# A third product on unscaled rows at each of four model-wide norms, and the scaling of the rows spread over it

## The reference

```python
def rmsnorm(x, g):
    xf = x.astype(jnp.float32)
    y = xf * lax.rsqrt(jnp.mean(xf * xf, axis=-1, keepdims=True) + EPS)
    return (y * g.astype(jnp.float32)).astype(x.dtype)
...
        hn = rmsnorm(h, mix_norm_g[l])
        proj = hn @ w_in[l]
        q_a, k_a, v_a, cq, ckv, k_pe = jnp.split(proj, IN_SPLITS, axis=-1)
...
        h = h + conv_glu(rmsnorm(h, ffn_norm_g[l]), w_gate[l], w_up[l], conv_w[l], conv_b[l], w_down[l])
...
        h = rmsnorm_2(x, norm_mix_g[l]) * (1.0 + sc_m) + sh_m
        proj = h @ w_in[l]
        a_b, a_c, a_x, q, f_logit, i_in, g_out, gate_a, gate_b = jnp.split(proj, split_idx, axis=-1)
...
        h2 = rmsnorm_2(x, norm_ffn_g[l]) * (1.0 + sc_f) + sh_f
        ff = (jax.nn.silu(h2 @ w_ffn_gate[l]) * (h2 @ w_ffn_up[l])) @ w_ffn_down[l]
```

## Time and profile before

| | |
|---|---|
| median of 3 runs | 2751.41 us (2748.62 to 2752.8) |
| the profiled execution | 2753.61 us, of it 2752.2 us span |
| PE busy | 97% of the span, mean granted clock 0.989 |
| DVE, ACT, POOL busy | 67%, 45%, 12% |

### The profile page before, as it was taken

The page is one execution under the profiler, slowest core; times in us unless marked ns, Lnnn a source line. Parts: engine busy times, 40 slices in busy tenths (PEclk is TensorE's granted clock), DMA queues, the critical chain, the costliest instruction groups (busy, mean ns, idle before and its releaser), DMA issues.

```text
span 2752.2 us, 51365 instructions
## 1 busy us (share of the span) xinstructions
PE 2677.2 (97%) x22052; PEld 2636.4 (96%) x22052; DVE 1836.5 (67%) x2578; ACT 1248.1 (45%) x1943; POOL 324.8 (12%) x526
## 2 busy tenths in 40 slices
PE   6999999899999999998999999999989999999998
PEld 6988889899999999998999999999989999999998
DVE  5656568777777777776888667766876445454444
ACT  5556555544433444445434443334544433344443
POOL 1110101111111111221000001111221000000001
PEclk9999999999999999999999999999999999999999
DMA  6433445688888888885444568886767556555553
GB/s 200 120 117 94 125 144 176 202 271 263 271 280 283 268 272 273 266 283 177 142 152 153 185 228 270 276 271 218 256 204 252 184 179 189 193 190 184 184 182 125
DMA packets 500084, 571.22 MB, mean 208 GB/s; under 512 B 26704, under 2 KB 473424, under 8 KB 499856
## 3 DMA queue, kind: packets, MB, share of 16 engines
q1 hardware_dynamic: 467968, 463.76, 51.9%
q0 software_dynamic: 31600, 103.80, 11.6%
q10 hardware_dynamic: 288, 0.36, 0.0%
HBM read 565.77 MB, written 2.54 MB: 206 GB/s over the span
## 4 chain that ended last, share of the span: by engine, by line
PE 86%; DVE 7%; ACT 4%; issue 1%; DMA 0%; POOL 0%; SPq 0%; DVEq 0%; ACTq 0%
PE ps L681 27%; PE ps L682 27%; PE ps L683 26%; DVE wl L1780 3%; ACT wh L1273 2%; PE ps L976 1%; PE ps L810 1%; DVE lr L1976 1%; DVE nx L1884 0%; ACT lp L1446 0%; DMA raw<-in_w_in 0%; PE ps L783 0%; DVE sqt L1884 0%; PE ps L835 0%; PE ps L836 0%
## 5 line engine op out<-in xcount | busy, mean ns | idle before, releaser
L1780 DVE TENSOR_TENSOR wl<-raw,wh 128x1024 fp32r<-128x1024 f32 (+1 forms) x894 | 1058.5, 1200 | 630.4 <-ACT wh L1273 626.2
L681 PE MATMUL ps<-xx,wh 128*128 128x256 f32 (+2 forms) x4848 | 1385.8, 286 | 29.2 <-DVE xx L1861 16.3
L682 PE MATMUL ps<-xx,wh 128*128 128x256 f32 (+2 forms) x4848 | 1366.4, 282 | 0.0
L683 PE MATMUL ps<-xx,wl 128*128 128x256 f32 (+2 forms) x4848 | 1363.1, 281 | 0.0
L1273 ACT ACTIVATE wh<-raw 128x1024 fp32r<-128x1024 f32 (+1 forms) x894 | 882.2, 1029 | 621.8 <-PE ps L683 612.3
L681 PEld LDWEIGHTS ps<-xx,wh 128*128 128x128 f32 x4848 | 918.0, 189 | 38.4 <-DVE wl L1780 21.9
L682 PEld LDWEIGHTS ps<-xx,wh 128*128 128x128 f32 x4848 | 918.9, 190 | 1.7 <-issue 1.0
L683 PEld LDWEIGHTS ps<-xx,wl 128*128 128x128 f32 x4848 | 918.4, 189 | 0.0
L681 PE MATMUL ps<-hid,wh 128*128 128x256 f32 x1408 | 393.9, 280 | 0.0
L682 PE MATMUL ps<-hid,wh 128*128 128x256 f32 x1408 | 393.7, 280 | 0.0
L683 PE MATMUL ps<-hid,wl 128*128 128x256 f32 x1408 | 392.8, 279 | 0.0
(11 more groups left out here) (366 smaller groups left out, 2387.4 us busy)
## 6 DMA issues: line engine op xcount, KB each, us to landing
raw<-in_w_in SPq DMA_DIRECT2D x118, 1024.0 KB, 5.3
ada_raw<-in_w_ada POOLq DMA_DIRECT2D x384, 256.0 KB, 4.7
raw<-in_w_gate SPq DMA_DIRECT2D x44, 1024.0 KB, 6.4
raw<-in_w_up SPq DMA_DIRECT2D x44, 1024.0 KB, 7.0
raw<-in_w_ffn_gate SPq DMA_DIRECT2D x44, 1024.0 KB, 5.1
raw<-in_w_ffn_up SPq DMA_DIRECT2D x44, 1024.0 KB, 5.6
raw<-in_w_down SPq DMA_DIRECT2D x32, 1024.0 KB, 6.6
raw<-in_w_ffn_down SPq DMA_DIRECT2D x32, 1024.0 KB, 5.5
```

Of the source, the lines that this page charges most:

```text
L681: pe.matmul(dst, h[:, c, o:o + w], x[:, 0, k, g.t0:g.t1], start=(k == 0), stop=False)
L682: pe.matmul(dst, h[:, c, o:o + w], x[:, 1, k, g.t0:g.t1], start=False, stop=False)
L683: m = pe.matmul(dst, l[:, c, o:o + w], x[:, 0, k, g.t0:g.t1], start=False, stop=end)
L1780: dve.tensor_tensor(wl[i % NS][:, part], raw[i % NR][:, part], wh[i % NS][:, part].bitcast(F32), ALU.subtract).then_inc(s_lo, 1)
```

## The change

At each of the four norms the third product is made raw too: `ckv` at N_IN, the second gate product of both feed-forward parts, and `i` at N_MIX2. The first product on scaled rows is the fourth one: `kpe`, which has 64 outputs and so 48 matmuls, the second up product, and `g`. For that

- the raw rows of three norms get buffers that outlast a third product (`raw_ffn` in two parts inside the space of `hid`, `raw_mix` for six chunks; chunks 6 to 15 of N_MIX2 still lie in `xx`, so that ScalarE may write the scaled high half of such a chunk only when the third product has passed it);
- `SCALE_AT` becomes a list with a pump for each chunk: one scaling a pump from pump 8 on for the feed-forward norms, where before four chunks took three pumps. ScalarE's high half of a chunk comes two pumps behind its scaling. VectorE's low half of an even chunk stays four chunks behind its scaling. GpSimd has its own count for odd chunks, three pumps behind the scaling;
- the third product's result is multiplied with `rstd` when it is read, by VectorE: two more reads for each norm (`unscaled`), with `keep_shift` for the shift product in the second block. `ckv` and `i`, which ScalarE copied out of PSUM, are now read by VectorE (for `i` ScalarE adds the shift behind it);
- `ada` is started or resumed one pair of products later in both feed-forward parts;
- the level masks are loaded to another place.

```diff
 def paced(n, i):
     if n in RAW_NORMS:
-        return pause((0, 1, 0, 2)[i % 4])
+        return pause(SCALE_AT[n][i + 1] - SCALE_AT[n][i] if i + 1 < KD else 2)
     return pause(i % 4 == 3)
...
-RAW_SHARED = {N_IN: [], N_FFN1: list(range(8, 16)), N_MIX2: list(range(16)), N_FFN2: []}
+RAW_SHARED = {N_IN: [], N_FFN1: [], N_MIX2: list(range(6, 16)), N_FFN2: []}
...
-RAW_KEY2 = {N_IN: ("cq", 1), N_FFN1: (1, "up", 0, 0), N_MIX2: ("f", 0), N_FFN2: (2, "up", 0, 0)}
+RAW_LAST = {N_IN: ("ckv", 0), N_FFN1: (1, "gate", 0, 1), N_MIX2: ("i", 0), N_FFN2: (2, "gate", 0, 1)}
...
-SCALE_AT = {N_IN: 10, N_FFN1: 8, N_MIX2: 8, N_FFN2: 6}
+SCALE_AT = {N_IN: [10, 11, 12, 13, 14, 15, 16, 17, 17, 18, 19, 20, 20, 21, 22, 23],
+            N_FFN1: [8 + i for i in range(16)],
+            N_MIX2: [10, 11, 12, 14, 16, 18, 19, 20, 21, 21, 22, 23, 24, 24, 25, 26],
+            N_FFN2: [8 + i for i in range(16)]}
...
-            gemm(("ckv", 0), normed(N_IN))
+            gemm_raw(N_IN, ("ckv", 0))
             lanes.start("latent", latent())
-            gemm(("kpe", 0))
+            gemm(("kpe", 0), normed(N_IN))
...
+                        elif f == 0 and g == 1:
+                            gemm_raw(n, (b, "gate", f, g))
+                            gemm((b, "up", f, g), normed(n))
                             if b == 1:
                                 lanes.start("ada", ada(), slow=True)
                             else:
                                 lanes.resume("ada")
...
-                    if p == 0 and n in "qf":
+                    if p == 0 and n != "g":
                         gemm_raw(N_MIX2, (n, p), square_sums if n == "q" else None)
...
                 if n in RAW_NORMS:
-                    yield from pause(SCALE_AT[n] + 1)
+                    yield from pause(SCALE_AT[n][1] + 3)
...
                     root(n)
-                    yield from pause(SCALE_AT[n] + 1 - ROOT_AT[n])
+                    yield from pause(SCALE_AT[n][0] + 2 - ROOT_AT[n])
...
+            dve.wait_ge(s_slab, done(("ckv", 0)))
+            for j in range(2):
+                unscaled(("ckv", 0), j, T, ckv[:, j, :])
             lanes.start("latent", latent())
```

More of the change, by code:

```diff
@@ L280 @@
 RAW_KEY = {N_IN: ("cq", 0), N_FFN1: (1, "gate", 0, 0), N_MIX2: ("q", 0), N_FFN2: (2, "gate", 0, 0)}
-RAW_T0 = {N_IN: Q0, N_FFN1: Q0, N_MIX2: Q0, N_FFN2: 0}
-RAW_T1 = {N_IN: T, N_FFN1: T, N_MIX2: T, N_FFN2: T - Q0}
-RAW_SHARED = {N_IN: [], N_FFN1: list(range(8, 16)), N_MIX2: list(range(16)), N_FFN2: []}
+RAW_T0 = {N_IN: Q0, N_FFN1: Q0, N_MIX2: 0, N_FFN2: 0}
+RAW_T1 = {N_IN: T, N_FFN1: T, N_MIX2: T - Q0, N_FFN2: T - Q0}
+RAW_SHARED = {N_IN: [], N_FFN1: [], N_MIX2: list(range(6, 16)), N_FFN2: []}
 RAW_LAG = {N_FFN1: {g: ([2 * g - 2, 2 * g - 1] if g < 7 else [12, 13, 14, 15]) for g in range(1, 8)},
@@ L470, in raw_half @@
                 return raw_in[:, h, i, :]
-            if n == N_FFN2:
-                return raw_ffn[:, h, i, :]
-            return xb[:, h, i, :] if n == N_FFN1 and i < 8 else xx[:, h, i, :]
+            if n == N_MIX2:
+                return raw_mix[:, h, i, :] if i < 6 else xx[:, h, i, Q0:T]
+            return raw_ffn[i // 8][:, h, i % 8, :]
         def raw_body(n, h, i):
@@ L481, in raw_shift @@
         def raw_shift(n, h):
[L482 to L485 removed]
+            if n == N_MIX2:
+                parts = [raw_mix[:, h, :, 0:META - Q0], xx[:, h, 6:KD, Q0:META]]
+            else:
+                parts = [x[:, h, :, 0:META - Q0] for x in raw_ffn]
+            m, c = (6, 0) if n == N_MIX2 else (8, 48)
+            cols = [mod[:, c:c + m], mod[:, c + m:c + KD]]
+            return [(x, y.unsqueeze(2).to_broadcast([P, k, META - Q0])) for x, y, k in zip(parts, cols, (m, KD - m))]
         def root_of(n):
@@ L624, in gemm_raw @@
                 t0, t1 = RAW_T0[n], RAW_T1[n]
+                if key == ("ckv", 0):
+                    t0 = 0
                 if key == (1, "up", 0, 0):
@@ L630, in gemm_raw @@
                 if NORM_SHIFT[n]:
-                    pe.wait_ge(s_shl, 1 if n == N_MIX2 else 2)
+                    pe.wait_ge(s_shl, 2 if n == N_MIX2 else 4)
                 for i in g.slabs:
@@ L652, in gemm_raw @@
                             m.then_inc(s_slab, 1)
-                        elif key == RAW_KEY2[n] and k in RAW_SHARED[n]:
+                        elif key == RAW_LAST[n] and k in RAW_SHARED[n]:
                             m.then_inc(s_passed, 1)
@@ L1070, in norm_lows @@
                     yield from paced(n, i)
+                    if n in RAW_NORMS and i + 1 < KD:
+                        yield from paced(n, i + 1)
             def squares(n, i):
@@ L1318, in pair_squares @@
                                 act.wait_ge(*last_use(("cq", g), j))
+                        act.wait_ge(s_slab, done(("ckv", 0)))
                     if n == N_CKV:
@@ L2338, in vector_program @@
                             dve.wait_ge(s_fq, j + 1)
+                            unscaled(key, j, SEQ, ssq["ab"[j]][:, 0:SEQ], META - Q0)
+                    if p == 0 and n == "i":
+                        dve.wait_ge(s_slab, done(key))
+                        for j in range(2):
+                            keep_shift(key, j, 4 + j)
+                            dve.wait_ge(s_fs, j + 1)
                             unscaled(key, j, SEQ, ssq["ab"[j]][:, 0:SEQ], META - Q0)
```

66 lines of the change are left out of this document (36 added, 30 removed).

## The result

The changed kernel takes 2722.57 us (median of 4 runs, 2720.61 to 2724.4) beside 2750.01 us (4 runs, 2746.86 to 2752.8) for the kernel before on the same chip. The ratio is 0.9898, 95% interval 0.9886 to 0.9910. The forecast was 2713, a gain of 38.6 us; measured are 28 by the ratio, 27.4 by the medians. The direction holds; the gain was forecast 10 us too large. The profiled execution took 2723.26 us with a span of 2721.9.

A forecast was written before the change was run, and what follows sets the result against it. TensorE, busy 97% of the span, was taken as the bound, with 46.9 us lost in four stalls; less 6.3 of remaining stalls and 2.0 of clock, the gain was 38.6 us, median 2713, range 2702 to 2731.

The forecast's parts named there:

- all is covered: Rival, 10%: waits for wh vanish and the key rotation's wait goes too, gain 49.0 us, so 2702.
- N_FFN1, chunk 12: Fourth product at N_FFN1: chunk 12 wanted at 31.4 us, its low half done at 34.1, a stall of 2.7 us.
- collisions: At N_FFN1, VectorE low halves beside GpSimd ones take 0.87 instead of 0.42 us; two on the path, 0.9 us.
- Stalls and the clock behind them: All four norms: 6.3 us of stalls left, plus 2.0 us for one half-clock stretch of 4 us.
- N_MIX2: stall of 1.6 us forecast: Second slab of g: chunk 12's low half waits behind wl, with four ScalarE roundings ahead of its wh; 1.6 us.
- N_FFN2: 1.0 forecast: As at N_FFN1, but third read-out 0.9 instead of 3.0 us and one more rounding per odd chunk: stall 1.0 us.
- N_IN: 1.0 forecast: At kpe, chunk 14 is wanted at 5.2 us and VectorE needs 5.5 to 6.5 before it: stall 1.0 us.
- It is not pushed into a wait later: At N_FFN2 the 2.7 us wait for ada_acc goes; ada's last group ends inside that part's first half.
- the forecast case: Main case, 62%: 2706 to 2719 us, its stalls between 3 and 12 us.
- the backlog is larger: Rival, 19%: all eight odd low halves collide, 14.4 us, and the clock falls at each stall, 8 us; gain 18, 2733.
- The wait moves: Rival, 5%: VectorE reaches wl late, TensorE waits for wl at line 648 or 681; gain under 5 us, 2748.
- the ring of five: Rival, 4%, slower: a scaling waits for GpSimd's low half five chunks back; 64 us lost instead of 46.9, 2768.

The follow-up runs named there:

- the best version: Changed kernel with later scalings earlier at three norms (N_MIX2's one pump more), all low halves on VectorE, ada's first start as before: 2710.26 us, 0.9843 of the kernel before.
- order: Changed kernel with other pump numbers alone, later scalings earlier at N_FFN1, N_MIX2 and N_FFN2: 2715.58 us, 0.9867 of the kernel before.
- after_again: The changed kernel unaltered, run once more as a control: 2724.65 us, 0.9897 of the kernel before.
- ada1: Changed kernel with ada in the first feed-forward part started behind the second product, as in the kernel before: 2720.72 us, 0.9887 of the kernel before.
- undo_ffn1: Changed kernel with N_FFN1 alone put back to two raw products, and ada's start with it: 2729.36 us, 0.9919 of the kernel before.
- lows_dve: Changed kernel with all 16 low halves of the four norms on VectorE, none on GpSimd: 2718.38 us, 0.9878 of the kernel before.
- the undo kernels: Changed kernel with one norm put back to two raw products: N_IN 2728.78, N_FFN1 2729.36, N_MIX2 2732.21, N_FFN2 2733.39 us.

## Why the prediction was right and where it was off

Between the profiled executions the gain is 2753.6 − 2723.3 = 30.3 us, 8.3 less than the 38.6 of the sum. The terms that it lies in: 5.0 us of stalls and half clock left at three norms, 2.0 given back between N_MIX2 and N_FFN2, and 1.1 at N_IN, which is inside the play of that part. The medians are 27.4 apart, since the profiled run before stood above its median by more than the one after.

- **What bounds the kernel: right.** TensorE stood still for low halves, and taking these waits away gave the time. The case "all is covered", 2702, is 8 us below the median of the best version.
- **The third raw product costs nothing: right**, 95 matmuls in 11 us.
- **N_FFN1, chunk 12: right in place and cause, low in size.** The second product starts at 482.3 us, chunk 12 is wanted at 513.5, 31.2 on (forecast 31.4), and its low half is done at 517.3, 35.0 on (forecast 34.1). Timeline of VectorE:

```profile
506.89 1.22 DVE L1798 TENSOR_TENSOR wl<-raw,wh 128x1024 fp32r<-128x1024 f32 x1
508.03 0.87 DVE L1881 TENSOR_TENSOR xx<-sqt,xx 128x258 fp32r<-128x258 f32 x1
...
512.33 0.41 DVE L1851 TENSOR_TENSOR ssq_a<-ps,rstd 128x258 f32<-128x258 f32 x1
...
515.32 1.22 DVE L1798 TENSOR_TENSOR wl<-raw,wh 128x1024 fp32r<-128x1024 f32 x1
516.45 0.87 DVE L1881 TENSOR_TENSOR xx<-nx,xx 128x258 fp32r<-128x258 f32 x1
```

  The read-out and its taps take 512.33 to 515.32, the forecast 3.0 us, and then a `wl` piece stands before the low half. In `order`, where the last low halves and their roundings stand ahead of it, the stall is gone, so their place is the cause. **The term of this ledger that was mis-sized is that of collisions**: two on the path, 0.9 us, were taken; 7 of 8 even low halves took 0.86 to 0.87 us, 3.1 us. It was partly made up by shorter waits for `wh`, 2.0 us where 3.0 were taken, and by the nine `wl` pieces, which follow each other at 1.14 us (506.89 to 508.03) and not at 1.2.
- **Stalls and the clock behind them.** The windows lose 5.2, 3.6 and 3.5 us, 12.3 in all, against 5.3 of stalls and 2.0 of clock in the forecast. Of the 5.0 us between, which are the largest part of what is missing, 3.6 are longer stalls (8.9 us) and 1.4 is the rest, for the most part half clock. One stretch of half clock, 3.4 us long, came at N_FFN1 (from 516.9, in the wait of 3.8 us) and one at N_FFN2 (from 2005.1, behind a wait of 1.9); the wait of 2.3 us at N_MIX2 brought none. In `after_again`, the same program, it was the other way round: a stretch at N_MIX2 behind a wait of 2.8 us, none at N_FFN2 behind one of 1.9. Its windows at N_MIX2 and N_FFN2:

```profile
1250.00:1290.00 40.00, 36.00 (x291) 35.64 (x290) 33.34 (x53) 27.18 (x45) 9.43 (x9) 0.96 0.54 177
1990.00:2030.00 40.00, 37.49 (x317) 37.11 (x316) 32.16 (x46) 24.45 (x37) 8.27 (x12) 1.00 0.67 220
```

- **N_MIX2: stall of 1.6 us forecast, 3.2 measured.** Chunk 12 was named, and waits 2.3; chunk 8 waits 0.9 and was missed. I had costed the roundings ahead of `wh`, not that ScalarE first stands 2.5 us at the read of `i`, which VectorE serves late.
- **N_FFN2: 1.0 forecast, 1.9 measured**, at chunk 12, and the half clock on top. Collisions are there as well, but on the scalings: 7 of 16 took 0.95 to 0.97 us beside a GpSimd low half, the others 0.47. One of each on VectorE, and the GpSimd low half beside the first:

```profile
1998.61 0.96 DVE L1902 SCALAR_TENSOR_TENSOR sqt<-H,small,rstd 128x256 f32<-128x256 f32 x1
1999.49 0.47 DVE L1902 SCALAR_TENSOR_TENSOR nx<-H,small,rstd 128x256 f32<-128x256 f32 x1
```

```profile
1998.33 0.95 POOL L1081 TENSOR_TENSOR xx<-sqt,xx 128x256 fp32r<-128x256 f32 x1 [1.86 <-ACT sqt L1382]
```

  At N_MIX2 three low halves and four scalings met one. How much of this is in the stalls of these two norms is not shown.
- **N_IN: 1.0 forecast; 1.0 and 0.2 measured.** The 1.0 is at the sums of the latent norm, behind the squares, the 0.2 at a low half. The wait for the key rotation stayed at 2.1 us, as said.
- **"It is not pushed into a wait later" was wrong.** With `ada` started a pair of products later, TensorE waits 1.3 us for it at 1940 us; `ada1` and `undo_ffn1`, where it starts as before, have no such wait. The steps that I followed were those of the resumed lane at N_FFN2; the later start at N_FFN1 was left out.
- **The signs to look for.** Waits for low halves 5 to 8 us: 9.3. None over 3.5: one of 3.8. At chunks 12 to 15: one was at chunk 8 of N_MIX2. Lost 1 to 4 us a norm: 5.2, 3.6 and 3.5. Clock above 0.95: 0.95, 1.00, 0.96. No wait for `wl` in second to fourth products: there is one of 1.3 us at the start of N_IN's second product (29.18 us), but the kernel before has it too, 1.4 us. No wait of line 1902 for GpSimd: so it was.
- **The rivals.** The time lies 3.6 us above the forecast case's own 2706 to 2719, toward "the backlog is larger" (2733). That one had the right mechanism: seven collisions came at each of N_FFN1, N_MIX2 and N_FFN2, where the forecast placed two on the path. What it had too large is their price: it left 28.7 us lost over four norms (6.3 + 14.4 + 8), while three windows lose 12.3 and the two new waits at N_IN are 1.2. "The wait moves" and "the ring of five" did not happen.
- **The rule held against the change.** The Trainium skill, "SBUF — State Buffer", section "SBUF: two separate sides": VectorE with two SBUF inputs and a GpSimd operation that reads SBUF lock each other out for a whole instruction. `lows_dve` agrees, 0.42 us each without GpSimd. I weighed that rule and then let my guess of two collisions carry the sum.

## What to carry to other kernels

When two engines share a list of short operations and one releases the other, they can run in step and meet nearly each time, here seven times for eight pairs at each of three norms: count a collision for every pair, look which operation it falls on, and ask whether the second engine saves anything at all. After moving work ahead of a deadline, look at what now stands between the last pieces of it and that deadline on each in-order engine; here other pump numbers alone, which put the read-out behind the last two low halves and their roundings, were worth 8 us, where the whole change was worth 28. And when lost time is read from a window, ask for each stall that is left whether half clock comes with it, and not once for all: here it came with two of three, and not with the same two in both executions of the changed kernel.

## What was not expected of the hardware

A low half on GpSimd also pays. Timeline of GpSimd in the changed kernel, one with VectorE idle beside it and one that begins under a `wl` piece:

```profile
491.08 0.65 POOL L1081 TENSOR_TENSOR xx<-nx,xx 128x258 fp32r<-128x258 f32 x1 [21.52 <-ACT xx L1397]
...
507.51 1.10 POOL L1081 TENSOR_TENSOR xx<-nx,xx 128x258 fp32r<-128x258 f32 x1 [1.61 <-ACT xx L1397]
```

Alone it takes 0.65 us. The second starts at 507.51, while the `wl` piece of 506.89 runs until 508.11, and ends at 508.61; the low half on VectorE from 508.03 ends at 508.90. So the ends fit a chain of `wl`, GpSimd and low half, each held by the one before. For the last step `lows_dve` shows it; for the first only these times speak. In `order`, where the low halves stand elsewhere, a scaling at N_FFN1 takes the blow instead, beside a GpSimd low half that runs from 507.27 to 509.11:

```profile
508.53 0.87 DVE L1902 SCALAR_TENSOR_TENSOR nx<-H,vec,rstd 128x258 f32<-128x258 f32 x1
```

The granted clock of the attention part is the other surprise: with the same instructions the half-clock stretches stand either near 100 us or between 160 and 250 us, and the sum of them before 480 us was 13.7 to 20.5 us in the traces of the kernels before and changed and the undo kernels. What decides between the two is open; it was not tried.
